# A layer's last query tile loaded once for both token tiles, and the even unit's fourth pair scored amid the odd unit's attention

## The reference, cut to what matters

```python
h = rms_norm(x, norm1_g[layer])
proj = h @ w_in[layer]                       # q, k, v of two attentions, forget logits, gates
y_diff = diff_attention(...)                 # 4 heads x 2 maps, causal
y_fox = forgetting_attention(...)            # 8 maps, causal
merged = sigmoid(ga) * (y_diff @ w_diff_o) + sigmoid(gb) * (y_fox @ w_fox_o)
x = x + merged @ w_out
x = x + peer_ffn(rms_norm(x, norm2_g[layer]), w_query, sub_keys, expert_u, expert_v)
```

## Time and profile before

| what | us or share |
|---|---|
| median of three runs | 2465.55 us |
| the profiled execution's own time | 2464.54 us |
| its span, first to last instruction | 2462.7 us |
| PE, DVE, ACT, POOL busy | 88%, 64%, 19%, 26% of the span |
| DMA, mean over the span | 366 GB/s, 900.95 MB |
| of it gathers (queue q0) | 537.43 MB |
| of it loads issued by SP (queue q1) | 357.95 MB |
| head, `attend(0)` | 0 to about 160 us |
| windows 1, 2, 3 | about 160 to 577, 577 to 995, 995 to 1412 us |
| last window, tail | 1412 to 1996, 1996 to 2463 us |

### The profile page before, as it was taken

How to read it: one execution, slowest core, us unless ns; L and a number is a source line. 1 busy time by engine, 2 the same in 40 slices (tenths; PEclk the granted TensorE clock), 3 DMA queues, 4 the chain that set the end, 5 groups by cost and what they waited for, 6 DMA issues and landing times. The chain is left out here.

```text
span 2462.7 us, 40094 instructions
## 1 busy us (share of the span) xinstructions
PE 2161.0 (88%) x16356; PEld 2003.0 (81%) x16356; DVE 1576.9 (64%) x4201; ACT 458.7 (19%) x986; POOL 636.5 (26%) x518
## 2 busy tenths in 40 slices
PE   9998899777889868788997798878998899999999
PEld 7887789777779868677896786878867798899799
DVE  1259588686778768868787888887688534212310
ACT  2211232101124011112301133100331012101100
POOL 0024334333334333433333313332233200000000
PEclk9999999989989989899998997989989999999999
DMA  8599999999999999999999988999989968568474
GB/s 316 198 387 421 421 421 418 422 421 420 421 418 417 421 411 421 416 422 416 385 421 420 421 350 325 405 424 384 409 332 401 423 240 367 189 240 313 166 257 154
DMA packets 107062, 900.95 MB, mean 366 GB/s; under 512 B 12765, under 2 KB 16897, under 8 KB 18177
## 3 DMA queue, kind: packets, MB, share of 16 engines
q0 software_dynamic: 73904, 537.43, 53.4%
q1 hardware_dynamic: 31872, 357.95, 36.7%
q10 hardware_dynamic: 1104, 3.02, 0.3%
HBM read 897.30 MB, written 1.05 MB: 365 GB/s over the span
## 5 line engine op out<-in xcount | busy, mean ns | idle before, releaser
L2454 POOL DMA_INDIRECT row<-in_experts,idx x448 | 559.1, 1248 | 1189.0 <-DVE acc L2016 552.9
L2033 DVE CUSTOM_DVE_ANT_0 row<-row,h2n 128x1024 f32<-128x1024 f32 x448 | 534.3, 1221 | 161.3 <-DMA row<-in_experts,idx 160.0
L915 PE MATMUL ea<-diag,row 128*128 128x128 f32 x3808 | 492.6, 294 | 137.4 <-DVE diag L2055 137.3
L915 PEld LDWEIGHTS ea<-diag,row 128*128 128x128 f32 x3808 | 481.0, 209 | 150.7 <-DVE diag L2055 149.0
L2016 DVE SCALAR_TENSOR_TENSOR acc<-row,wgt,acc 128x1024 f32<-128x1024 f32 x207 | 265.2, 1281 | 2.0
L1521 ACT ACTIVATE gl<-dots 128x4 f32<-128x4 f32 x128 | 26.3, 206 | 918.5 <-DVE dots L2033 918.4
L997 PE MATMUL pa<-hB,wring 128*128 128x144 f32 (+1 forms) x1056 | 149.5, 306 | 34.9 <-DMA wring<-in_weights 32.2
L997 PEld LDWEIGHTS pa<-hB,wring 128*128 128x128 f32 x1056 | 145.3, 210 | 38.7 <-DMA wring<-in_weights 34.0
L997 PE MATMUL ea<-hB,wring 128*128 128x144 f32 (+1 forms) x1056 | 137.4, 293 | 3.4 <-DMA wring<-in_weights 3.4
L997 PEld LDWEIGHTS ea<-hB,wring 128*128 128x128 f32 x1056 | 135.2, 198 | 4.2 <-DMA wring<-in_weights 3.8
L807 PE MATMUL pa<-hA,wring 128*128 128x128 f32 x960 | 123.1, 281 | 0.0
(11 more groups left out here) (546 smaller groups left out, 3245.7 us busy)
## 6 DMA issues: line engine op xcount, KB each, us to landing
wring<-in_weights SPq DMA_DIRECT2D x110, 2048.0 KB, 11.7
wlate<-in_weights SPq DMA_DIRECT2D x25, 2048.0 KB, 8.3
wring<-in_weights SPq DMA_DIRECT2D x22, 1408.0 KB, 6.6
wlate<-in_weights SPq DMA_DIRECT2D x10, 1408.0 KB, 6.3
more<-in_weights SPq DMA_DIRECT2D x5, 2048.0 KB, 8.3
row<-in_experts,idx POOLq DMA_INDIRECT x448, 18.5
row<-in_weights SPq DMA_DIRECT2D x3, 2048.0 KB, 16.9
...
```

The costliest lines, as they stand in the source:

```text
L915: m = pe.matmul(EA[c // 4][:, (c % 4) * P:(c % 4 + 1) * P], v[:, c * P:(c + 1) * P], diag[:, DIAG_SLOTS * (q % 2) + i, :], start=False, st ...
L2033: dve.tensor_tensor_reduce(out=r, in0=r, in1=h2n[:, u % 2, :], scale=1.0, scalar=0.0, op0=ALU.mult, op1=ALU.add, accum_out=dots[:, g % 2, ...
L2454: pool.indirect_dma_start(out=expert_rows[slot], out_offset=None, in_=table, in_offset=bass.IndirectOffsetOnAxis(ap=idx[:, k % 3, GB * g + ...
```

## The change

Tile 17 (now called `SHARED`) isn't loaded for an even unit, and the even unit makes no wq3 and no s3. The odd unit loads it between tiles 11 and 12 and uses it twice: first on token tile 0 (`xq3`, with `x0raw`, the gained x of token tile 0, which DVE makes in the memory of `prob`), then on its own tokens (wq3). ACT copies the query to `qT`, PE multiplies it with the keys (`xs3`, L787 of the new kernel), and ACT writes `keys[:, 3]` with the even unit's norm factor, kept in `st[:, 14:15]`. The even unit's fourth pair is picked from there. As tile 17 stays in its place from xq3 to wq3, tiles 12, 13, 14 and then 15 of an odd unit all go through the other place (`places`). In unit 0 rows 6 to 9 alone are taken by early tiles.

The tables change too. The `SLOT` table of odd units starts its projections closer together (two steps in slot 0 and two in slot 1), has the maps in slots 6 to 14 instead of 8 to 16, fo0 and fo1 in slot 15, do and xq3 in 16, xs3 and out0 in 17, out1 in 18, wq3 with st2 in 19, wq0 in 20, wq1 in 24, wq2 in 26 and s3 in 28. The `DENSE` slots of windows 1 and 3 are now 0 to 4, 15 to 19 and 24. For the fourth pair of an even unit `best_keys` moves one group later and shares it with `best_pairs`.

```diff
-GROUPS_A = (["st1", "dq", "bc1", "dk", "dv", "fq", "fk", "ff", "fv"] + [f"gate{t}" for t in range(4)]
-            + ["dst", "fo0", "dbc", "fo1", "do0", "do1", "out0", "out1", "st2", "wq0", "s0", "hn0", "hn1"]
-            + ["wq1", "wq2", "s1", "wq3", "s2", "s3"])
...
+GROUPS_A = (GROUPS_HEAD + ["out0", "out1", "st2", "wq0", "s0", "hn0", "hn1", "wq1", "wq2", "s1", "s2"],
+            GROUPS_HEAD + ["xq3", "xs3", "out0", "out1", "st2", "wq3", "wq0", "s0", "hn0", "hn1", "wq1", "wq2", "s1", "s2", "s3"])
...
+SHARED = TILES1 - 1
+TILES_T = (list(range(SHARED)), list(range(12)) + [SHARED] + list(range(12, SHARED)))
+STREAM1 = [(u, t) for u in range(UNITS) for t in TILES_T[u % 2]]
...
+def places():
+
+    out, turn = [], 0
+    for u, t in STREAM1:
+        if u == 0:
+            out.append(RING + EARLY1.index(t) if t in EARLY1 else t % RING)
+        elif t in (12, 13, 14) and u % 2:
+            out.append(1 - kept)
+        else:
+            if t == SHARED:
+                kept = turn
+            out.append(turn)
+            turn = 1 - turn
+    return out + [(turn + k) % 2 for k in range(DEPTH * TILES2 + 2)]
...
-DENSE = (0, 1, 5, 6, 7, 21, 22, 25, 30)
+DENSE = ((0, 1, 2, 3, 4, 15, 16, 17, 18, 19, 24), (0, 1, 5, 6, 7, 21, 22, 25, 30), (0, 1, 2, 3, 4, 15, 16, 17, 18, 19, 24))
...
+        if k in (PAIRS - 1, 3 * PAIRS - 1):
+            turns = [q + 3, q + 3, q + 4, q + 5]
...
 SLOT = ([0, 1, 2, 3, 4, 5, 6, 7] + [8 + i // 2 for i in range(MAPS + 2)]
-        + [17, 18, 19, 20, 21, 22, 23, 24] + [25, 26, 28, 30])
-STEPS_A = len(SLOT)
+        + [17, 18, 19, 20, 21, 22, 23, 24] + [25, 26, 28, 30],
+        [0, 0, 1, 1, 2, 3, 4, 5] + [6 + i // 2 for i in range(MAPS + 2)]
+        + [15, 15, 16, 16, 17, 18, 19, 20] + [21, 22, 24, 26, 28])
...
+                def key_products(name, t):
+
+                    b = group(name)
+                    for hp in range(4 * t, 4 * t + 4):
+                        m = pe.matmul(b[:, hp % 4 * P:(hp % 4 + 1) * P], qT[:, hp, :], kcol[:, hp % 2, :], start=True, stop=True)
+                    return m
...
+                if tt:
+                    features("xq3", weights(SHARED, KC), 0, x0raw, KC, ("a_xr", {0: 3, 4: 4}))
+                    yield
+                    T.evacuated(pe, "xq3")
+                    T.inc(key_products("xs3", 3), "a_pj")
...
-                w, b = weights(14, KC), group("wq0")
+                w, b = (weights(SHARED, KC), group("wq3")) if tt else (weights(14, KC), group("wq0"))
...
                 queries(2)
                 key_scores(1)
                 yield
-                queries(3)
                 key_scores(2)
-                key_scores(3)
+                if tt:
+                    key_scores(3)
...
+                if tt:
+                    T.wait(act, "a_fo", 2)
+                    out("xq3", qT[:, 12:16, :])
+                    yield
+                    if u >= 3:
+                        act.wait_ge(e_idx, 2 * (PAIRS * (u - 2) + 3) + 2)
+                    Tile(u - 1).wait(act, "a_r", 3)
+                    out("xs3", keys[:, 3, :], scale=st[:, 14:15])
...
+                    if group == "st2" and tt == 0:
+                        stt(st[:, 14:15], st[:, 4:5], 1.5, st[:, 2:3], ALU.add, ALU.mult)
...
+                if tt:
+                    T.wait(dve, "a_o", DH + FH)
+                    for hf in range(2):
+                        gained(C1_N2, hf, x0raw, tokens_of(0))
...
-                    Tile(u).evacuated(dve, f"s{t}")
+                    if t == 3 and u % 2 == 0:
+                        Tile(u + 1).evacuated(dve, "xs3")
+                    else:
+                        Tile(u).evacuated(dve, f"s{t}")
```

More of the change, by code:

```diff
@@ L64 @@
 NK2 = K2_MASK + T2
-GROUPS_A = (["st1", "dq", "bc1", "dk", "dv", "fq", "fk", "ff", "fv"] + [f"gate{t}" for t in range(4)]
-            + ["dst", "fo0", "dbc", "fo1", "do0", "do1", "out0", "out1", "st2", "wq0", "s0", "hn0", "hn1"]
-            + ["wq1", "wq2", "s1", "wq3", "s2", "s3"])
-NG = len(GROUPS_A)
-GA = {n: i for i, n in enumerate(GROUPS_A)}
-FREED = {"bc1": ("a_h", KC + 1), "dbc": ("a_y", 1), "fo0": ("a_fo", 1), "fo1": ("a_fo", 2),
-         "do0": ("a_do", 1), "do1": ("a_do", 2), "out0": ("a_x", 1), "out1": ("a_x", 2)}
@@ L73 @@
-EVACS = [n for n in GROUPS_A if n not in FREED]
-FREED.update({n: ("a_evac", i + 1) for i, n in enumerate(EVACS)})
-PER_TILE = {"a_pj": NG, "a_evac": len(EVACS), "a_sq": 5, "a_s": MAPS, "a_t": DH + FH, "a_o": DH + FH, "a_e": MAPS,
-            "a_pt": DH + FH, "a_or": DH + FH, "a_misc": 2, "a_h": KC + 1, "a_xr": 4, "a_sr": MAPS, "a_p": MAPS, "a_y": 3,
+UNITS = 2 * DEPTH
+GROUPS_HEAD = (["st1", "dq", "bc1", "dk", "dv", "fq", "fk", "ff", "fv"] + [f"gate{t}" for t in range(4)]
+               + ["dst", "fo0", "dbc", "fo1", "do0", "do1"])
@@ new lines @@
+GROUPS_A = (GROUPS_HEAD + ["out0", "out1", "st2", "wq0", "s0", "hn0", "hn1", "wq1", "wq2", "s1", "s2"],
+            GROUPS_HEAD + ["xq3", "xs3", "out0", "out1", "st2", "wq3", "wq0", "s0", "hn0", "hn1", "wq1", "wq2", "s1", "s2", "s3"])
+GA = [{n: i for i, n in enumerate(groups)} for groups in GROUPS_A]
+FREED_DVE = {"bc1": ("a_h", KC + 1), "dbc": ("a_y", 1), "fo0": ("a_fo", 1), "fo1": ("a_fo", 2),
+             "do0": ("a_do", 1), "do1": ("a_do", 2), "out0": ("a_x", 1), "out1": ("a_x", 2)}
+EVACS = [[n for n in groups if n not in FREED_DVE] for groups in GROUPS_A]
@@ L96, in loads1 @@
 def loads1(place, n):
-    return sum(place1(m) == place for m in range(n))
+    return PLACE1[:n].count(place)
 TURNS_E = UNITS * PAIRS
@@ L489, in window_order @@
                         yield
-                    while step < len(SLOT) and SLOT[step] <= slot:
+                    while step < len(SLOT[w % 2]) and SLOT[w % 2][step] <= slot:
                         next(a)
@@ L839, in key_scores @@
                     T.evacuated(pe, f"wq{t}")
-                    b = group(f"s{t}")
-                    for c in range(4):
-                        hp = 4 * t + c
-                        m = pe.matmul(b[:, c * P:(c + 1) * P], qT[:, hp, :], kcol[:, hp % 2, :], start=True, stop=True)
-                    T.inc(m, "a_pj")
+                    T.inc(key_products(f"s{t}", t), "a_pj")
                 def head_scores(h):
@@ L1816, in attend @@
                     dve.wait_ge(a_cols, 16 * (l + 1))
-                    Tile(u - 1).filled(dve, "wq3")
+                    Tile(u - 1).filled(dve, "wq2")
                 if u >= 2:
```

84 lines of the change are left out of this document (49 added, 35 removed).

## The result

The kernel after took 2494.43 us (median of five runs, 2490.97 to 2496.82), against 2465.55 (2462.98 to 2469.85) for the kernel before: a ratio of 1.0117, 95% interval 1.0102 to 1.0133, or 28.9 us slower. The prediction was 2461.6 with a range of 2453 to 2474. It was wrong, in size and in sign. One of the twelve executions of a later run, e16, took 3477.21 us at a mean granted clock of 0.56, and its ratio leaves that execution out.

What follows compares the result with a forecast made beforehand. Bytes at a 421 GB/s DMA ceiling were taken to bound windows 1 to 3, PE the head. One tile less, -4.98, plus 2 x 0.5 for waits gave -4.0: 2460.5 profiled, 2461.6 as median, range 2453 to 2474.

Steps and rivals of the forecast that it cites:

- the single place: Out1 in odd windows: PE waits 4.1 us for tile 13, mostly hidden by queued gathers; 0.5 us each, bounds 0 and 4.1.
- the ledger: Odd windows' slots 15 to 20: PE work 78.4 us against DMA's 89.6, so cover shrinks to 11.2 us; cost 0.
- The queue of gathers: At out1's wait in odd windows: DMA has over 10 us of gathers in hand, which hides the 4.1 us.
- The bytes: Window 2, bound by DMA, loads one tile less for unit 2: -4.98 us.
- Unit 0's tile: Head: one tile less to load there, taken as 0 us; at most 2.3 us gained.
- the first gelu: Window 1's start: a sign that it comes near 170, with the first gather staying at 155.7.
- The moved start: Odd windows' maps move to slots 6 to 14: value 0, bounds -6.9 and +6.9 us on window 3's shortfall.
- DVE's term: Odd windows: more dense slots and bunched picks in slot 18, lateness caught up; value 0, bounds 0 and 4 us per window.
- D: Rival: rows run dry in odd windows' slots 15 to 20, each losing 9.5 us; 2479.6 us, chance 0.10.
- PE's room stays positive: Argument against the rows-run-dry rival: in slots 15 to 20 DMA still wants 11.2 us more than PE, 7.1 after the wait.
- E: Rival: the wait at out1 lowers PE's clock, out1 takes 7.31 us more in each odd window; 2476.2 us, chance 0.07.
- C: Rival: the wait for tile 13, 4.1 us per odd window, isn't hidden and eats the gain; +3.2, 2468.8 us, chance 0.13.

Runs made afterwards that it cites:

- e16: Kernel before with every odd-unit step two slots earlier, the first four in slots 0, 0, 1, 1; bytes, tiles, picks and dense slots unchanged: 2470.55 us, 1.0022.
- e4: Kernel before with odd units' tiles 13 and 14 loaded into tile 12's place, so tile 13 waits for out0's end; all else kept: 2465.21 us, 0.9999.
- e1: Kernel after with the shared tile loaded twice in odd units, so no place is kept, at one tile more per odd window: 2482.17 us, 1.0075.
- e12: Kernel before with ten instead of twelve places for gathered expert rows: 2471.28 us, 1.0031.
- e8: Kernel before with only 128 of 4096 columns of unit 2's last query tile loaded (weights left out, no candidate): 2459.82 us, 0.9982.
- e13: Kernel after with xq3 and xs3 behind out1, directly ahead of wq3, no place kept, dense slots of before, later picks: 2466.59 us, 1.0007.
- e5: Kernel after with the dense slots of the kernel before in every window; steps, picks and kept place stay: 2485.56 us, 1.0081.

## Why the prediction was wrong

**The step that failed** is the place's term, "the single place", 0.5 us per odd window, and beside it the ledger (the sum of work) of slots 15 to 20, 78.4 us of PE against 89.6 of DMA. Measured, that stretch took PE 99.2 us. The ledger had summed products and left out every wait, even the 8.40 us one for st2's squares that stood in my own. With them: 78.4 + 8.0 (out1) + 7.25 (st2) + 2.1 and 0.3 (xq3, fo1) + 3.0 and 2.1 (the groups behind the two long waits, slow) = 101.2, near the 99.2 of window 1 (window 3: 97.0); neighbouring groups overlap a little in the trace. That is over DMA's 89.6 and not under it; the rates say 14.6 and 12.9 us of idle DMA there. I compared PE's work with DMA's. What competes is PE's chain, waits and all. In the old steps the kept place is free, as e4 shows; in a stretch that has no room for it, it costs some 20 us over two windows (e1), and not 1.0.

**The size of the wait.** I took 8.0 us between out0 and out1 from the earlier trace rows. Of that gap 2.56 us was PE waiting for a diagonal and 5.46 three rows; after, only two rows, 3.6 us of the gap, stand there. The tile came 11.6 us after out0's end (438.71 - 427.1), inside the 11.3 to 13.0 of the earlier trace rows, and 11.6 - 3.6 leaves 8.0, not 4.1.

**The empty slot.** Before, the chain has seven slots, 17 to 23, and slot 23 holds only expert rows, so PE catches up there. After, a chain with 8.4 us more work (xq3 and xs3) has six slots. I compared six slots with six.

**The queue of gathers** hid waits where PE could catch up afterwards. In e4, with 12.9 us a slot, it hid all of it, 6.4 and 7.8 us with their slow products. In the kernel after too little is caught up, since the slots of the chain take 16.5 us on average against DMA's 15; one by one, from row block to row block in window 1, they are some 20, 12, 22, 21 and 11 us. That the queue is no free cover shows in e12: two places fewer, 7.6 us.

**The bytes** were right where I put them: -4.4 us in e8, and window 2 shorter by 7.8 (2.3 MB, 5.5 us, and its 3.0 of idle time). But in the kernel after, the end of window 3 takes most of the tile back. The next block's constants (`k2st`, 1.25 MB) are issued in the odd unit's last step, now in slot 28 and not 30, and land ahead of the border. The queue that carries them, in window 3, before and after:

```profile
q10 hardware_dynamic: 63, 0.14, 0.1%
```
```profile
q10 hardware_dynamic: 288, 1.53, 0.9%
```

That moves 1.39 MB, 3.3 us, out of window 4, where DMA isn't full, into window 3, where it is. e13 has the same 1.53 MB, which may be why its full windows don't beat before; no run put that load back, so this is argued from bytes and not shown.

**The head, the start and DVE.** Unit 0's tile gave nothing that shows, as said: the first gather was issued at 155.83 (155.69 before), the first gelu came at 173.45 and not near 170, and from 157 to 197 us, in tens, DMA moved 351, 424, 418 and 420 GB/s (365, 421, 422 and 417 before). The moved start, which I had at 0, costs some 5 us alone (e16). DVE's term was 0, with bounds of 0 and 4 us a window; giving back the dense slots in it was worth 9 us in all (e5), 4.5 a window, so this term was too small as well, though no trace shows where they lie.

**The rivals.** D named the right place and sign: rows run dry in slots 15 to 20, by its own test of a DMA share below 0.97 (0.88 measured). Its price, 9.5 us a window, was two thirds of the stretch's 14.6 and 12.9; its chance of 0.10 was far too low, because "PE's room stays positive" rested on the same ledger. E's clock is part of the sum, 5 us in window 1, and costs nothing alone (e4). C's wait of 4.1 us was half of the 8.04 and 7.85 that came, and its sum, +3.2 us, had nothing else in it.
